# Norms between chained matmuls: two tiles per VectorE instruction, mean subtracted on VectorE, the last down tile and the next projection cut by token halves in another order

## The reference, cut to what matters

```python
def _rms(x):                      # block 1, layer 0: retention/delta mixer, layer 1: RG-LRU mixer
    return x * lax.rsqrt(jnp.mean(x * x, -1, keepdims=True) + 1e-6)
h = h + mixer(rms_norm(h, norm_mix[layer]))            # norms 0 and 2
h = h + conv_ffn(rms_norm(h, norm_ffn[layer]))         # norms 1 and 3, d_ff 2816
h = rms_norm(h, norm_final)                            # norm 4
# block 2, l = 0, 1; alpha = 4 ** 0.25
x = _layer_norm(alpha * x + 0.5 * _swiglu(x, w_gu[l, 0], w_down[l, 0]), g0, b0)   # norms 5, 8
x = _layer_norm(alpha * x + _token_mixers(x, ...), g1, b1)                        # norms 6, 9
x = _layer_norm(alpha * x + 0.5 * _swiglu(x, w_gu[l, 1], w_down[l, 1]), g2, b2)   # norms 7, 10
```

## Time and profile before

| | us |
|---|---|
| median of 3 runs | 3750.05 |
| lowest, highest | 3732.88, 3797.62 |
| the profiled execution | 3772.73 |
| its span, first to last instruction | 3770.9 |
| PE busy in it | 3550.4 |
| DVE, ACT, POOL busy | 1848.0, 1415.4, 78.0 |

### The profile page before, as it was taken

The page is one execution under the profiler, slowest core; times in us unless marked ns, Lnnn a source line. Parts: engine busy times, 40 slices in busy tenths (PEclk is TensorE's granted clock), DMA queues, the critical chain, the costliest instruction groups (busy, mean ns, idle before and its releaser), DMA issues.

```text
span 3770.9 us, 47195 instructions
## 1 busy us (share of the span) xinstructions
PE 3550.4 (94%) x16820; PEld 2879.4 (76%) x16820; DVE 1848.0 (49%) x2802; ACT 1415.4 (38%) x2309; POOL 78.0 (2%) x97
## 2 busy tenths in 40 slices
PE   7978799999799999999999989999999999989997
PEld 6858678887688888888766678887888776678886
DVE  4576666535566534334454553335333445553335
ACT  3341344324544323222445443224222445442323
POOL 0000000000000000000000010001000100010001
PEclk9999999999899999999979599999999999589998
DMA  3210122232222232222210022222323220012222
GB/s 128 78 51 1 58 87 97 94 99 75 73 85 96 96 99 86 99 96 95 79 33 1 12 73 97 98 96 81 100 95 98 83 78 1 1 56 95 96 98 98
DMA packets 89741, 288.48 MB, mean 77 GB/s; under 512 B 9968, under 2 KB 14576, under 8 KB 89072
## 3 DMA queue, kind: packets, MB, share of 16 engines
q1 hardware_dynamic: 89440, 284.69, 22.7%
q0 software_dynamic: 144, 1.70, 0.1%
HBM read 284.26 MB, written 2.10 MB: 76 GB/s over the span
## 4 chain that ended last, share of the span: by engine, by line
PE 85%; DVE 7%; ACT 3%; issue 3%; DMA 1%; DVEq 0%; ACTq 0%; SPq 0%
PE gb L535 23%; PE gb L536 23%; PE gb L537 23%; PE gb L1038 4%; PE pm L1067 3%; PE pm L1054 2%; DMA wst<-in_weights 1%; DVE wl L1625 1%; DVE xl L1663 1%; PE gb L855 1%; ACT h L1171 1%; PE gb L594 1%; PE gb L593 1%; PE gb L595 1%; PE pm L864 1%
## 5 line engine op out<-in xcount | busy, mean ns | idle before, releaser
L535 PE MATMUL gb<-xh,wh 128*128 128x512 f32 (+1 forms) x3104 | 1198.9, 386 | 95.4 <-DVE xl L1663 68.3
L536 PE MATMUL gb<-xl,wh 128*128 128x512 f32 (+1 forms) x3104 | 1179.4, 380 | 0.0
L537 PE MATMUL gb<-xh,wl 128*128 128x512 f32 (+1 forms) x3104 | 1178.9, 380 | 0.0
L1625 DVE TENSOR_TENSOR wl<-wst,wh 128x1024 fp32r<-128x1024 f32 (+3 forms) x600 | 646.0, 1091 | 569.8 <-ACT wh L1126 563.2
L1126 ACT CAST wh<-wst 128x1024 fp32r<-128x1024 f32 (+3 forms) x600 | 555.8, 942 | 636.2 <-DMA wst<-in_weights 635.7
L535 PEld LDWEIGHTS gb<-xh,wh 128*128 128x128 f32 x3104 | 594.8, 192 | 225.0 <-DVE xl L1663 70.0
L536 PEld LDWEIGHTS gb<-xl,wh 128*128 128x128 f32 x3104 | 595.4, 192 | 109.2 <-issue 2.2
L537 PEld LDWEIGHTS gb<-xh,wl 128*128 128x128 f32 x3104 | 594.4, 191 | 107.6
L535 PE MATMUL gb<-hid,wh 128*128 128x512 f32 (+2 forms) x1212 | 447.5, 369 | 5.5 <-DVE wl L1625 5.5
L536 PE MATMUL gb<-hid,wh 128*128 128x512 f32 (+2 forms) x1212 | 444.4, 367 | 0.0
L537 PE MATMUL gb<-hid,wl 128*128 128x512 f32 (+2 forms) x1212 | 444.2, 367 | 0.0
(11 more groups left out here) (341 smaller groups left out, 3067.5 us busy)
## 6 DMA issues: line engine op xcount, KB each, us to landing
wst<-in_weights SPq DMA_DIRECT2D x408, 512.0 KB, 3.3
wst<-in_weights SPq DMA_DIRECT2D x84, 384.0 KB, 2.9
wst<-in_weights SPq DMA_DIRECT2D x84, 320.0 KB, 3.0
h<-in_x_t SPq DMA_DIRECT2D x2, 1024.0 KB, 6.3
out_t<-h SPq DMA_DIRECT2D x8, 256.0 KB, 2.3
tab<-in_first SPq DMA_DIRECT2D x1, 1984.0 KB, 15.2
wst<-in_weights SPq DMA_DIRECT2D x20, 96.0 KB, 2.2
tab<-in_second POOLq DMA_DIRECT2D x1, 1664.0 KB, 7.6
```

The costliest lines, as they stand in the source:

```text
L535: pe.matmul(dst, w_hi, x_hi, start=start, stop=False)
L536: pe.matmul(dst, w_hi, x_lo, start=False, stop=False)
L537: return pe.matmul(dst, w_lo, x_hi, start=False, stop=stop)
L1625: dve.tensor_tensor(wl[:, s, m, a], wst[:, s, m, a], f32(wh[:, s, m, a]), ALU.subtract).then_inc(lo_split, 1)
```

## The change

- The mean is subtracted on VectorE (`centred`), and POOL's loop is gone.
- Subtraction, scaling and (where the norm's result stays in `h`) the low part take two tiles per instruction. In RMS norms the gain moves to ScalarE's cast and into VectorE's low part.
- The reciprocal of half 1 comes after all of half 0. `late` stands between the tiles.
- The two splits of the next projection's first chunk move from the stage before into half 0 of the norm; the first up steps split one half each of chunk c0+2.
- `one_by_half` replaces `pair_by_half`: for each token half the first output half runs over all tiles, then the second. The sums of half 1 stand behind the first output half of token half 0. The second chunk follows directly.
- `down_last` goes by token half outside, over both chunks. Its sums of half 0 stand after the first quarter of half 1.
- ScalarE's warm-up of the root's table moves from ahead of the down product to behind its second tile.

Core of the diff (the functions of before are printed above; ScalarE's part first, then VectorE's, and the LRU and first mixer have the same edits as the up steps):

```diff
-ROOT_AT, SPLIT_AT = 4, 4
...
-            with pool.Fori(0, 3 * LAYERS) as i:
-                for v, t in enumerate(HV):
-                    pool.wait_ge(mean_ready, 2 * i + v + 1)
-                    for k in range(1, KT):
-                        pool.tensor_tensor(h[:, k, t], h[:, k, t], mu2[:, t], ALU.subtract).then_inc(off_ready, 1)
...
+            def one_by_half(c, n, ln_run):
                 for v, t in enumerate(HV):
-                    for k in range(KT):
-                        pe.wait_ge(xl_ready, 16 * n + 8 * v + k + 1)
-                        for m in range(2):
+                    for m in range(2):
+                        if v == 0:
+                            wait_half(c, m)
+                        for k in range(KT):
+                            if m == 0:
+                                pe.wait_ge(xl_ready, 8 * n + 4 * v + k // 2 + 1)
                             col = slice(k * P, k * P + P)
-                            mm = three(gb[:, 2 * p + m, t], wh[:, 0, m, col], wl[:, 0, m, col], xh[:, k, t], xl[:, k, t],
+                            mm = three(gb[:, m, t], wh[:, 0, m, col], wl[:, 0, m, col], xh[:, k, t], xl[:, k, t],
                                        k == 0, k == KT - 1)
-                            if v == 1 and k == KT - 1:
-                                mm.then_inc(chunk_done if m else half_done, 1)
-                        if v == 0 and k == 0 and not isinstance(ln_run, str):
-                            sums(n, ln_run, 1)
+                            if v == 0 and m == 0 and k == KT - 1 and not isinstance(ln_run, str):
+                                sums(n, ln_run, 1)
+                        if v == 1:
+                            mm.then_inc(chunk_done if m else half_done, 1)
+                pair(c + 1, None, 1, 1, x_of)
...
-                wait_group(g0)
-                pair_by_half(c0, 0, n - 1, ln_in)
-                pair(c0 + 1, g0 + 1, 1, 1, x_of)
+                pe.wait_ge(group_free, g0)
+                one_by_half(c0, n - 1, ln_in)
...
-                    for s in range(2):
-                        for q in range(2):
-                            wait_half(c + s, q)
-                        for v, t in enumerate(HV):
+                    for v, t in enumerate(HV):
+                        for s in range(2):
                             for q in range(2):
+                                if v == 0:
+                                    wait_half(c + s, q)
                                 for k in range(DOWN[q]):
                                     f, cols = s * HALF + q * DOWN[0] + k, slice(k * P, (k + 1) * P)
                                     mm = three(gb[:, 2 + v, t], wh[:, s, q, cols], wl[:, s, q, cols],
                                                hid[:, 0, f, t], hid[:, 1, f, t], f == 0, f == FT - 1)
                                 if v == 1:
                                     mm.then_inc(chunk_done if q else half_done, 1)
-                                    if s == 1 and q == 0:
+                                    if s == 0 and q == 0:
                                         sums(n, ln_run, 0)
-                            if s == 1 and v == 0:
-                                mm.then_inc(S("down_half"), 1)
+                        if v == 0:
+                            mm.then_inc(S("down_half"), 1)
...
+            def split_half(c, s, m, cols=COLS):
+                act.wait_ge(w_in[s][m], 8 * (c - s) + 16)
+                act.copy(wh[:, s, m, 0:cols], wst[:, s, m, 0:cols]).then_inc(hi_split, 1)
             def split_hi(c, s, cols=(COLS, COLS)):
                 for m in range(2):
-                    act.wait_ge(w_in[s][m], 8 * (c - s) + 16)
-                    act.copy(wh[:, s, m, 0:cols[m]], wst[:, s, m, 0:cols[m]]).then_inc(hi_split, 1)
+                    split_half(c, s, m, cols[m])
...
+            def norm(n, ln=None, gain=None, final=False, k_ln=None, late=None, late_at=2, first=None, split=None):
+                def high(j, v):
+                    t, pair_ = HV[v], slice(2 * j, 2 * j + 2)
+                    act.wait_ge(xf_ready, 8 * n + 4 * v + j + 1)
+                    for k in (2 * j, 2 * j + 1):
+                        if ln is not None:
+                            ins = act.activation(h[:, k, t], h[:, k, t], ACT.Identity, scale=lay[:, 16 * k_ln + k:16 * k_ln + k + 1],
+                                                 bias=lay[:, 16 * k_ln + 8 + k:16 * k_ln + 9 + k])
+                        elif final:
+                            ins = act.activation(h[:, k, t], h[:, k, t], ACT.Copy, scale=prm[:, gain + k:gain + k + 1])
+                        else:
+                            ins = act.activation(xh[:, k, t], xf[:, k % 2, HV[j % 2]], ACT.Copy, scale=prm[:, gain + k:gain + k + 1])
+                    if ln is None and not final:
+                        ins.then_inc(xh_ready, 1)
+                        return
+                    base = 0 if final else 8 * (n - 4)
+                    ins.then_inc(ln_out, 1)
+                    act.wait_ge(ln_out, base + 4 * v + j + 1)
+                    act.copy(xh[:, pair_, t], h[:, pair_, t]).then_inc(xh_ready, 1)
                 norm_root(n, ln, 0)
+                if first:
+                    split_half(*first, 0)
+                for j in range(KT // 2):
+                    high(j, 0)
+                    if first and j == 0:
+                        split_half(*first, 1)
+                    if late and j == late_at:
+                        late()
+                norm_root(n, ln, 1)
+                for j in range(KT // 2):
+                    high(j, 1)
+                    if j == 1 and split:
...
-                split_hi(c0 + 4, 0)
...
                 def up(j, s):
                     c, e = c0 + j, run * FT + j
-                    if not (isinstance(j, int) and j == 0):
+                    if not isinstance(j, int):
                         split_hi(c + 1, 1 - s)
+                    elif j == 0:
+                        split_half(c + 2, 0, 0)
                     act.wait_ge(chunk_done, c + 1)
...
                 up(0, 0)
+                split_half(c0 + 2, 0, 1)
                 up(1, 1)
                 with act.Fori(1, FT // 2) as i:
                     for s in range(2):
                         up(2 * i + s, s)
-                root_ready()
                 for m in range(KT):
                     for s in range(2):
-                        split_hi(c0 + FT + 2 * m + s + 1, 1 - s, DOWN_COLS if 2 * m + s < 2 * KT - 1 else (COLS, COLS))
+                        if 2 * m + s < 2 * KT - 1:
+                            split_hi(c0 + FT + 2 * m + s + 1, 1 - s, DOWN_COLS)
...
+                    if m == 1:
+                        root_ready()
...
+            def norm(n, ln=None, final=False, gain=None, late=None, late_at=1, first=None, split=None):
                 in_h = final or ln is not None
+                def two(j, v):
+                    return h[:, 2 * j:2 * j + 2, HV[v]]
+                def centred(j, v):
+                    if ln is not None:
+                        dve.wait_ge(mean_ready, 2 * (n - 5) + v + 1)
+                        dve.tensor_tensor(two(j, v), two(j, v), over_tiles(mu2[:, HV[v]], 2), ALU.subtract).then_inc(off_ready, 1)
+                def variance(v):
                     t = HV[v]
                     if ln is not None:
                         i = n - 5
                         dve.wait_ge(sq_summed, 2 * n + v + 1)
                         dve.wait_ge(d2_ready, 2 * i + v + 1)
                         dve.scalar_tensor_tensor(rt[:, t], stat2[:, t], 1.0 / D, xf[:, 0, t], ALU.mult, ALU.subtract).then_inc(var_ready, 1)
+                        centred(0, v)
+                def inverse(v):
+                    t = HV[v]
                     dve.wait_ge(rt_ready, 2 * n + v + 1)
                     dve.reciprocal(rinv[:, t], rt[:, t]).then_inc(rinv_ready, 1)
+                def scaled(j, v):
                     t = HV[v]
+                    if j == 0:
                         dve.wait_ge(rinv_ready, 2 * n + v + 1)
+                    else:
+                        centred(j, v)
                     if ln is not None:
+                        dve.wait_ge(off_ready, 8 * (n - 5) + 4 * v + j + 1)
+                        dst = two(j, v)
+                    elif final:
+                        dst = two(j, v)
                     else:
+                        dst = xf[:, :, HV[j % 2]]
+                        if 4 * v + j >= 2:
+                            dve.wait_ge(xl_ready, 8 * n + 4 * v + j - 1)
+                    dve.tensor_tensor(dst, two(j, v), over_tiles(rinv[:, t], 2), ALU.mult).then_inc(xf_ready, 1)
+                def low(j, v):
                     t = HV[v]
+                    dve.wait_ge(xh_ready, 8 * n + 4 * v + j + 1)
+                    if in_h:
+                        pair_ = slice(2 * j, 2 * j + 2)
```

(31 more changed lines are left out.)

147 lines of the change are left out of this document (50 added, 97 removed).

## The result

| | before | after |
|---|---|---|
| median of 20 runs each, us | 3757.2 | 3771.04 |
| lowest and highest, us | 3714.8, 3809.21 | 3751.37, 3803.24 |
| profiled execution, us | 3772.73 | 3797.22 |
| ratio after / before, 95% interval | | 1.0085 [1.0053, 1.0117] |

The changed kernel is slower by 14 us in the medians and by 0.85% (32 us) in the ratio, which leaves out executions far above the fastest of their kernel; forecast were 3774 us and +24. The profiled execution has +24.5 us, but that number is the sum of a loss in the norms and a gain in stages that the change doesn't touch, as the pieces show.

What follows compares the result with a forecast made beforehand. Bound: matrix engine busy 94%, so only gaps in eleven norms (9 to 17 us each), set by VectorE's order. Terms +16 and clock +8 gave +24 on 3772.7: 3797, or 3774 us on the median; range 3755 to 3795.

Steps and rivals of the forecast that it cites:

- First pieces: Last residual tile's start to first reciprocal's end: changes of −5.85 (norm 2), −3.95 (5, 8), −1.25 (1, 3), −1.3 us (6, 9).
- The serial chain between the halves: Second reciprocal waits for half 1's sums, VectorE mostly idle: 6.4 us in layer norms, 3.75 in RMS norms.
- The halves on VectorE: Half 0 11.7 us in layer norms (12.8 behind output), 9.6 in RMS (10.15); half 1 11.8 and 8.6.
- Middle pieces: First reciprocal's end to last low part: layer norms 29.9 and 31.0 us (before 26.4, 26.9), RMS 21.95 and 22.5.
- The clock: Half-rate matmuls: from nothing to 20 us (last 24 matmuls of nine norms at half rate); +8 us taken.
- last piece: Last low part to the second chunk's first 512-column matmul: 3.6 us in every norm (before 2.1, 1.0, 1.8, 1.7).
- Down entries: Root's table load moves behind the down product's second tile: 1.6 of a 1.74 us wait goes, −3.2 us in two FFNs.
- The sum: Norm terms and the moved table load together +16 us; with +8 for the clock, +24 on the profiled execution.
- The earlier start is passed on: Rival, 28%: the first output half stays fed, so the middle's added 3.5 us vanish; 3734 us, 3718 without half-rate stretches.
- Slower by more, the clock: Rival, 9%: matrix engine at 1.2 GHz in both halves, layer norms' sums 4.8 for 2.4 us; +34 on +16, 3800 us.

Runs made afterwards that it cites:

- experiment 3: Changed kernel with the last down tile back in the old order (both token halves, chunk half by chunk half); median 3804.2 us, ratio 1.0180 against the kernel before.
- experiment 2: Changed kernel with early sums: half 1's sums behind the first tile pair, its variance, root and reciprocal inside half 0; median 3732.8 us, ratio 1.0025.
- the hybrid: Changed kernel with early sums; half 0 keeps its output order, half 1 takes both output halves per tile; median 3706.0 us, ratio 0.9948.
- experiment 1: Changed kernel with both output halves following each arriving tile in a projection's first chunk; median 3753.5 us, ratio 1.0080 against the kernel before.
- both and early with the split back: As both and early, with the first weight split behind output projections ahead of the tail's squares again; median 3721.3 us, ratio 0.9941.
- both and early: Changed kernel with the edits of experiment 1 and experiment 2 together; median 3719.4 us, ratio 0.9899 against the kernel before.
- experiment 4: Changed kernel with the mean subtracted on POOL again for pairs 1 to 3 of each half, two tiles per instruction; median 3816.8 us, ratio 1.0220.

## Why the prediction was right, and where it wasn't

The direction and the mechanism (longer middle and last pieces against shorter first ones) came out, but the hit of 3774 for 3771 has luck in it: the kernel before itself came out at 3757 beside it, not at 3750, so the difference was 14 us for 24 in the medians and 32 in the ratio. Point by point:

- **First pieces: right.** 13.4 for down with RMS (forecast 13.4), 12.0 for output with RMS (12.05), 15.24 for down with layer norm (15.7), 13.8 for output with layer norm (14.4). The down order alone is 3.96 us per down norm (experiment 3), as 33 × 0.120 had it.
- **The serial chain between the halves: right, but too short.** From the last low part of half 0 (1813.19) to the second reciprocal's end (1820.06) are 6.9 us in norm 5, forecast 6.4; experiment 2 takes it away and the gain is there. In norms 6, 8 and 9 it is 8.2, 7.5 and 8.2: the sums themselves take 3.2 to 3.8 us there, 2.5 in norm 5. In the RMS norms 1, 2 and 3 it is 5.5, 5.3 and 4.9 where I had 3.75. In norm 2 the twelve matmuls of the last two pairs run at half rate up to the sums, and I had left the clock out of this term:

```profile
862.96 0.58 PE L528 MATMUL gb<-xh,wh 128*128 128x256 f32 x1 [1.88 <-DVE xl L1703]
865.68 0.84 PE L612 MATMUL pm<-sq,com 128*128 128x256 f32 x2
```

- **The halves on VectorE: right.** Half 1 of a layer norm 11.4 for 11.8, of an RMS norm 8.84 for 8.6; half 0 from 1801.95 to 1813.19 = 11.2 for 11.7. Middle pieces together are 269.7; the forecast's add up to 261.0 if norm 10 is taken like norm 7, and the chains' excess over 6.4 and 3.75 (9.6 us in seven norms) accounts for the difference.
- **The clock: the mis-sized term.** I had 0.7 + 2.9 = 3.6 for the last piece of every norm and +8 us for the clock over the whole kernel. The last pieces are 3.7 to 6.1, 51.7 in ten norms for 36: +15.7, of which 138 matmuls at half rate make 13.1 (0 to 23 of the 30 or so behind the last low part of each norm). With the chains' 9.6, which I put down mostly to the clock as well without having measured its share in each, that is some 25 us, over my upper bound of 20, which had the last 24 matmuls of nine norms at half rate and nothing between the halves. The row at 0.215 us in the earlier trace rows was the evidence, and I gave it less than half its weight because the kernel before "already pays part of that". It paid little: in norm 5, 15 of its last 24 matmuls ran at half rate, not all, in the other norms at most nine of those behind the last low part, and its last pieces were 0.9 to 2.5 us.
- **Down entries: right.** The matrix engine waits 0.33 us where the earlier trace rows had 1.74; the stages from norm 1 to 2 and 3 to 4 are 1.4 and 2.9 shorter (forecast 1.6 each).
- **The sum.** My terms for the norms came to +19, with the clock +27; measured +39.3. What brings the profiled executions to the forecast +24 is the mixer stages' −12.4, which no step of mine held. The norms' part is too small by 12, and that the two errors cancelled is luck.
- **Rivals.** "The earlier start is passed on" is half true: experiment 3 shows that it is, but the chain of 6.4 us took it back, as its "against" said; in experiment 2 and the hybrid, where the chain is gone, the medians are 3733 and 3706, where that rival had put 3734 and 3718. "Slower by more, the clock" was the better account of the last pieces, and half true of both halves too: norm 5 ran at half rate from 1808.52 to 1814.48, and the layer norms' sums took up to 3.8 us, in the second execution of the same kernel 4.5 in norm 5, where it had put 4.8 for 2.4.

## What to carry to other kernels

When a producer engine sets the pace, what follows its last piece of work should be as little as possible: a second pass over the same tiles is free in the first half, where the matrix engine waits anyway, and costs its whole length (here partly at half clock) in the last. When an instruction order is made coarser (8 tiles, then the sums), ask for each small result inside whether another engine's chain begins with it; moving the sums, with the steps that feed and use them, from behind the eighth tile to behind the second was worth 46 us in the norms, the largest effect in this study. And before two single edits are combined, check which later input the combined order makes the first step wait for.

## What the runs showed of the hardware

- TensorE fell to 1.2 GHz in the middle of work whose single waits were short. In half 0 of norm 5 the changed kernel had waited 1.06 us twice (1805.90 and 1807.95) before it, in half 1 it had waited 3.37 and 0.95 us (1823.44 and 1825.37), each time with six matmuls between. It was back at 2.4 GHz at 1835.54, after 18 matmuls in one run. "TensorE: Matmul & The Clock Gate" in the Trainium skill (part 1) tells it as idleness throttling and activity releasing; the rows agree with that direction. With both outputs per tile (experiment 1) norm 5 waited 6.22 us, ran 24 matmuls at 1.2 GHz from 1819.58, and its last 24, from 1825.77, at 2.4 GHz.
- The two mixer stages, the same code in every kernel here, took 323 to 380 us each from one execution to the next, at granted clocks of 0.78 to 0.96, with the other engines' busy time unchanged. A profile's total is then no measure of a change of 1%; its pieces are, for the part that they cover. The lowest runs order the kernels nearly as the norms' sums do: 423, 448, 452, 458, 459, 481 and 498 us for the hybrid, both and early with the split back, early sums, both and early, the kernel before, both outputs and the changed kernel, with lowest runs of 3674, 3700, 3697, 3701, 3700, 3737 and 3751 us (of before over all comparisons).
- A VectorE subtraction of 512 columns took 1.75 us beside POOL's and 0.68 without (experiment 4), a reciprocal of 256 columns 1.74 and 1.75.
